# Inverse roots of the second and third feed-forward block by two transfers through DRAM instead of four transposes

## The reference

```python
def rmsnorm(x, g):
    xf = x.astype(jnp.float32)
    y = xf * lax.rsqrt(jnp.mean(xf * xf, axis=-1, keepdims=True) + EPS)
    return (y * g.astype(jnp.float32)).astype(x.dtype)

def conv_ffn(x, w_up, conv_w, conv_b, w_down):      # w_up: 1024 x 5632
    S = x.shape[1]
    u = x @ w_up
    u_pad = jnp.pad(u, ((0, 0), (CONV_WIDTH - 1, 0), (0, 0)))
    hc = conv_b
    for j in range(CONV_WIDTH):                       # width 3, causal
        hc = hc + conv_w[j] * u_pad[:, j:j + S]
    a, b = split_cols(hc, (FFN_DIM, FFN_DIM))         # 2816 each
    return (jax.nn.silu(a) * b) @ w_down

h = h + conv_ffn(rmsnorm(h, norm_ffn[i]), w_up[i], conv_w[i], conv_b[i], w_down[i])
```

## Time and profile before

| | |
|---|---|
| median of 3 runs | 2060.12 us (2059.34 to 2060.75) |
| the profiled execution | 2060.0 us |
| its span, first to last instruction | 2058.2 us |
| mean granted TensorE clock | 0.999 of full speed |
| HBM read, written | 187.45 MB, 6.03 MB |

### The profile page before, as it was taken

How to read it: one execution, slowest core, us unless ns; L and a number is a source line. 1 busy time by engine, 2 the same in 40 slices (tenths; PEclk the granted TensorE clock), 3 DMA queues, 4 the chain that set the end, 5 groups by cost and what they waited for, 6 DMA issues and landing times.

```text
span 2058.2 us, 29716 instructions
## 1 busy us (share of the span) xinstructions
PE 2041.5 (99%) x10035; PEld 1664.9 (81%) x10035; DVE 971.6 (47%) x1719; ACT 576.5 (28%) x1145; POOL 1276.0 (62%) x846
## 2 busy tenths in 40 slices
PE   9999999999999999999999999999999999999998
PEld 7888778788888887899888888888875588888887
DVE  5452464655552055566455555334367535555311
ACT  3211433422220054323342222000247632222100
POOL 7666638866667668332666666666555566666663
PEclk9999999999999999999999999999999999999999
DMA  5222473323233342211123323334410033232332
GB/s 190 92 92 92 113 107 118 108 92 99 95 107 108 102 147 94 73 62 42 62 92 92 101 92 102 103 103 143 148 42 2 11 99 96 92 102 92 103 103 81
DMA packets 56259, 195.09 MB, mean 95 GB/s; under 512 B 6355, under 2 KB 6803, under 8 KB 55924
## 3 DMA queue, kind: packets, MB, share of 16 engines
q1 hardware_dynamic: 49536, 177.78, 27.4%
q10 hardware_dynamic: 6644, 16.25, 3.5%
HBM read 187.45 MB, written 6.03 MB: 94 GB/s over the span
## 4 chain that ended last, share of the span: by engine, by line
PE 60%; DVE 1%; ACT 1%; issue 0%; DVEq 0%; ACTq 0%
PE acc L855 16%; PE acc L859 16%; PE acc L858 16%; PE acc L1144 2%; PE sc L1161 2%; PE pp L1180 2%; PE acc L1397 1%; PE acc L927 0%; PE pp L1176 0%; DVE s_m L2102 0%; PE acc L1089 0%; PE pp L1375 0%; PE acc L1319 0%; PE pp L1376 0%; PE sc L1375 0%
## 5 line engine op out<-in xcount | busy, mean ns | idle before, releaser
L728 POOL TENSOR_TENSOR wlo<-wraw,whi 128x1024 fp32r<-128x1024 f32 x332 | 802.2, 2416 | 27.7
L726 POOL TENSOR_SCALAR whi<-wraw 128x1024 fp32r<-128x1024 f32 x332 | 351.9, 1060 | 625.0 <-PE acc L855 575.1
L855 PE MATMUL acc<-xhi,whi 128*128 128x512 f32 x1752 | 686.3, 392 | 4.5 <-POOL wlo L740 2.8
L859 PE MATMUL acc<-xlo,whi 128*128 128x512 f32 x1752 | 682.0, 389 | 0.0
L858 PE MATMUL acc<-xhi,wlo 128*128 128x512 f32 x1752 | 681.9, 389 | 0.0
L855 PEld LDWEIGHTS acc<-xhi,whi 128*128 128x128 f32 x1752 | 328.9, 188 | 77.2 <-DVE xlo L1683 5.2
L859 PEld LDWEIGHTS acc<-xlo,whi 128*128 128x128 f32 x1752 | 328.9, 188 | 68.9
L858 PEld LDWEIGHTS acc<-xhi,wlo 128*128 128x128 f32 x1752 | 329.0, 188 | 67.1
L855 PE MATMUL acc<-fhi,whi 128*128 128x512 f32 x528 | 205.4, 389 | 0.0
L858 PE MATMUL acc<-fhi,wlo 128*128 128x512 f32 x528 | 205.4, 389 | 0.0
L859 PE MATMUL acc<-flo,whi 128*128 128x512 f32 x528 | 205.4, 389 | 0.0
(11 more groups left out here) (406 smaller groups left out, 2407.1 us busy)
## 6 DMA issues: line engine op xcount, KB each, us to landing
wraw<-in_weights SPq DMA_DIRECT2D x331, 512.0 KB, 3.5
distances<-vr ACTq DMA_DIRECT2D x1, 3840.0 KB
toep<-distances ACTq DMA_DIRECT2D x4, 768.0 KB, 8.5
mem<-in_mem_t ACTq DMA_DIRECT2D x2, 1024.0 KB, 15.1
w<-in_weights ACTq DMA_DIRECT2D x1, 2048.0 KB, 10.4
h<-in_x_t SPq DMA_DIRECT2D x3, 512.0 KB, 7.7
out_t<-h SPq DMA_DIRECT2D x6, 256.0 KB, 2.4
dmf<-in_sums ACTq DMA_DIRECT2D x1, 576.0 KB, 5.9
```

What stands on the lines that cost most here:

```text
L726: nc.gpsimd.tensor_scalar(whi[:, j, :], wraw[:, j % RAW, :], 1.0, 1.0, ALU.mult, ALU.mult).then_inc(sem["w_hi"], 1)
L728: nc.gpsimd.tensor_tensor(wlo[:, j, :], wraw[:, j % RAW, :], plain(whi[:, j, :]), ALU.subtract).then_inc(sem["w_split"], 1)
L855: m = nc.tensor.matmul(o, a_hi, b_hi, start=start, stop=False)
L859: m = nc.tensor.matmul(o, a_hi, b_lo, start=False, stop=stop)
```

## The change

In the second and third feed-forward block the four transposes of `root_t` and DVE's copy of their result are gone. In their place ACT, behind its square root and DVE's reciprocal, issues a transfer of `root_t` into a DRAM tensor of 512 numbers in the order of the tokens, waits for its end, and issues a second transfer that reads this row into `rstd` on all 128 partitions. DVE waits for the second one, where it waited for the transposes. After its reciprocal DVE also tells PE that `pv` is free (`rs_taken`), which its copy did before. The memset of `u` stands ahead of the roots in all three blocks. The waits on `rs_ready` count two fewer in the end. The first block, the final normalisation and all others keep their transposes.

```diff
+    carried_roots = nc.dram_tensor("carried_roots", [1, S], F32, kind="Internal").ap()
...
             squares, roots = lambda: sum_features(KD), lambda: spread_roots(root_t)
-            spread(xhi, xlo, between={4: squares, 7: roots} if squared else None)
+            spread(xhi, xlo, between={4: squares} if squared else None)
...
         def factor(to):
 
-            dve.wait_ge(sem["rs_ready"], rs)
+            dve.wait_ge(sem["rs_ready"], rs - carried)
             n.did(V.tensor_copy(to, pv[:, 0:to.shape[-1]]), sem["rs_taken"])
+
+        carried = 0
...
+        def roots_carried():
+
+            nonlocal carried
+            invert()
+            n.tell(sem["rs_taken"])
+            carried += 1
+            dve.wait_ge(sem["roots_in"], 16 * carried)
...
         def feed_forward(which):
 
-            roots(rstd)
             did(V.memset(u[:, :, 0:2], 0.0))
+            if which == "ffn0":
+                roots(rstd)
+            else:
+                roots_carried()
...
+        def carry():
+
+            nonlocal carried
+            carried += 1
+            act.wait_ge(sem["rq_ready"], bc)
+            act.dma_start(carried_roots.rearrange("o (i p) -> p (o i)", p=P), root_t[:, :], allow_slow_non_contiguous=True).then_inc(sem["roots_out"], 16)
+            act.wait_ge(sem["roots_out"], 16 * carried)
+            act.dma_start(rstd[:, :], carried_roots.to_broadcast([P, S])).then_inc(sem["roots_in"], 16)
+
+        carried = 0
...
             squares([h[:, KD - 1, :]], sqbanks)
             ahead(gain, 4, KD)
             root(D)
+            carry()
 
         entry("nffn1")
```

More of the change, by code:

```diff
@@ L557, in build_program @@
              "gates_ready hid_raw act_step in_row in_mem0 in_mem1 z_done hi_ready kpe_ready cs_ready q_copied e_copied fm_ready fh_ready "
-             "dm_ready la_raw lah_ready ml_ready me_ready mn_ready mt_ready mc_ready gn_ready o_ready keys_done mv_ready mo_hi mo_ready zeroed ya_ready ya_taken fin_ready fin_roots fin_done").split()
+             "dm_ready la_raw lah_ready ml_ready me_ready mn_ready mt_ready mc_ready gn_ready o_ready keys_done mv_ready mo_hi mo_ready zeroed ya_ready ya_taken fin_ready fin_roots fin_done roots_out roots_in").split()
     sem = {n: ctx.enter_context(nc.semaphore(n)) for n in names}
```

## The result

| | before | after |
|---|---|---|
| median | 2060.43 us (6 runs, 2059.34 to 2061.95) | 2069.78 us (6 runs, 2066.83 to 2071.52) |
| ratio | | 1.0044, 95% interval 1.0033 to 1.0055 |
| the profiled execution, its span | 2060.0, 2058.2 us | 2071.2, 2069.4 us |

The change makes the kernel 9.4 us slower. Its six runs lie 4.7 us apart, those of before 2.6; the one that was profiled lies 1.4 us above their median. The page of the changed kernel begins with the same picture as the earlier trace rows: PE at 99%, but the chain that ended last now has transfers in it.

A forecast was written before the change was run, and what follows sets the result against it. PE was taken as the bound, so removing the transposes saves 0.94 us over two blocks and all else costs nothing: 2060.0 - 0.94 = 2059.06, plus 0.12 for the median, hence 2059.2 us; range 2058.0 to 2061.5.

The forecast's parts named there:

- What bounds the kernel: Whole kernel: PE is busy 99% of the span; other engines' work counts only if PE comes to wait for it.
- The transposes, 0.47 us per block: PE's stream, second and third feed-forward block: removing four fp32 transposes saves 0.47 us each, 0.94 us in all.
- The budget of 12.2 us: Changed blocks: rstd may land up to 12.2 us behind the reciprocal's end before PE waits for its bank.
- The write, 1.9 to 7.4 us: ACT's transfer of root_t to DRAM, 512 elements of 4 bytes: lands in 1.9 to 7.4 us, taken as 4.6.
- The read, 2.1 to 5.0 us: Transfer from DRAM to rstd, 256 KB: lands in 2.1 to 5.0 us, taken as 3.2.
- The weight stream costs nothing: Weight loads beside the new transfers: 5.2 us of slack cover the new traffic, PE untouched, cost nothing.
- Rival 1: Changed blocks: slow write, at 0.35 us an element rstd at 1064.4, PE waits 4.3 us twice, 2067.8 us; chance 7%.

The follow-up runs named there:

- spaced_write: The change with its 512 elements written 64 bytes apart in DRAM, the second transfer reading a row of input x instead: 2058.97 us, ratio 0.9993.
- m1: A program of transfers only, small writes and reads in several forms, alone and beside weight loads; the change's write landed in 10.2 us alone, first round.
- read_only: The change without its write, the second transfer reading a row of input x instead of the roots: 2059.76 us, ratio 0.9998.
- write_alone: The kernel before, transposes kept, plus the write of the roots to DRAM, not waited for inside the blocks: 2060.24 us, ratio 1.0001.

## Why the prediction was wrong

- **What bounds the kernel**: right. PE is the bound, and what happened is told by PE's waits alone.
- **The transposes, 0.47 us per block**: right; the stream is 15.03 - 14.56 = 0.47 us shorter.
- **The budget of 12.2 us**: right. rstd came 15.5 us behind the reciprocal in the second block, 3.3 over it, and PE waited 3.1; in the third it came after 17.1, 4.9 over it, and PE waited 4.7.
- **The write, 1.9 to 7.4 us**: this is the step that failed. The upper end let each element cost as much as a mean packet, 5.5 us in all, on top of the shortest landing. That took the engines' time for the landing time. The packets cost only 9 ns each, and yet the landing was 10.2 and 11.7 us, because the elements are 4-byte neighbours in DRAM: 64 bytes apart they landed in 4.5 and 3.7 (spaced_write). No row of before has such a write, and the bound was drawn from packets of over 2 KB. It should have been called no bound: where the form of a transfer is new in the way its pieces lie to each other, the packet time says nothing of it.
- **The read, 2.1 to 5.0 us**: the upper end came, not the 3.2 I took. It takes 3.0 us alone and 4.5 to 5.9 beside a constant stream of weight loads (m1). In the change it ran beside the weight load that the write had made late; with the pieces of 16 bytes it landed in 3.1 to 3.3. A late load is not needed for it, though: read_only has no write, and its read took 5.1 and 4.3.
- **The weight stream costs nothing**: right (write_alone).
- **Rival 1** happened: rstd at 1064.4 was its price, PE waiting 4.3 us twice; 3.1 and 4.7 came. Its mechanism, an element that costs over 0.29 us, was wrong, since 128 elements take nearly as long as 512 (7.1 and 8.3 us). Its time, 2067.8, lacked the slow products. I gave it 7%, on the strength of the bound that was none.
- **The clock** was in no step: a wait of PE was priced at its own length. In the profiled execution 7.8 us of wait brought 4.4 us of slow products with them, more than half as much again. The terms that the sum lacked are the waits that the write made (7.8 us) and these slow products.

## What to carry to other kernels

Before a detour through DRAM is priced, look at how the pieces of the write lie to each other: elements of 4 bytes that are neighbours in DRAM but come one by one landed here in 7 to 12 us, the same numbers in pieces of 16 bytes in 1.4 to 4, and undoing the order in the reader's access pattern was free. Price a stall of PE above its length, since the products behind it may run at half clock. And weigh the two sides: the saving was 0.47 us per place, the forecast left the chain of two transfers 4.2 us of slack, and missing it cost 3.1 and 4.7 us of wait and the slow products on top.

## What the runs showed of the hardware that I had not expected

- The landing of a small write into DRAM goes with the distance between the starts of its pieces: 1.4 to 1.9 us at 16 bytes and more, 2.7 to 3.0 at 8 bytes, 6.9 to 8.3 at 4 bytes (medians; up to 12.1 beside other traffic), nearly the same for 128 and for 512 elements.
- A transfer of 528 packets can be over on the engines 3.2 us after its issue and land after 10.2 (alone 1.3 and 8.6), and weight loads beside it land after 6.1 and 8.2 us instead of 3.6.
- TensorE's granted clock fell to 1.2 GHz after idle times of 2.9, 3.1 and 4.7 us between products, for 6, 7 and 12 products (those whose rows show 0.63 us or more), and did not after 1.3 us or 0.2 us.
- A DVE product with an operand read in steps of 16 bytes took 1.06 us instead of 0.69.
